# Expert tail of a two-block kernel: last down slabs in column halves, residual kept aside, one input slab loaded later

## The chip, the cores and the metric

The kernel runs on one core of one Trainium2 chip. Its time is the device time of one execution in microseconds (us), and the number compared is the median of several executions. Engines: PE (TensorE), DVE (VectorE), ACT (ScalarE), POOL (GpSimd) and SP (SyncE); the last two issue most of the DMA transfers. Each engine works through its own instructions in the order written.

## The reference, cut to what matters

Two transformer blocks run one after the other on 256 tokens of width 1024, in float32. The first ends in a mixture of 32 experts, top 2 per token:

```python
a = jnp.einsum('nd,edf->nef', t, w_gate)          # 32 experts, 1024 -> 256
b = jnp.einsum('nd,edf->nef', t, w_up)
hid = jax.nn.silu(a) * b * combine[:, :, None]
routed = jnp.einsum('nef,efd->nd', hid, w_down)   # 256 -> 1024
ffn = routed + shared
h = h + rms_norm(ffn, post_ffn_norm)              # end of the first block
...
h = rmsnorm(x, norm_mix_g)                        # start of the second block
proj = h @ w_in                                   # 1024 -> 7168
```

All expert weights (96 slabs of 1 MB: a gate, an up and a down matrix of each expert) are read from memory. Then follow the second block's projections, recurrence, attention, MLP and final norm, none of which the change alters in what they compute.

## The kernel before

**Experts.** They go in eight groups of four (`QUADS`, q = 0 to 7). A group has 12 slabs: four gate, four up, four down. They live in a ring of 12 slots of the big buffer, and slab n may be loaded once the slab 12 before it is used up (`expert_slab_used`). Even slabs are issued on SP's queue, odd ones on POOL's (L442). For each group PE multiplies the gate slabs (L2215, 64 records), the up slabs (L2215), turns the hidden values (L2222), multiplies the down slabs (L2229, 32 records, which write PSUM banks 2 and 3), and adds the result into the sum of the tokens by a matmul with the routing weights (`combine`, L2236, 8 records), after ACT (L935) and DVE (L1563) copied the two banks to `yrow`. `keep_busy` (L2126) are matmuls whose result nobody reads; group 7 has 16 of them between gate and up.

**From the first block to the second.** The token sums lie in PSUM banks 4 to 7, two banks for each half `t` of the tokens. ACT squares them and takes the root (L976, L979); DVE scales by the root and by the norm's weight `gain_ffn` (L1652) and adds the residual, a scaled copy of `h_tok` read with a stride (L1656). That completes `ffn_tmp` and counts up `h_ffn`. ACT squares again (L983), DVE normalizes to `h2n` (L1662), PE transposes it (L2137). ACT and DVE then write the high and low parts of each of eight column chunks (L990 into XH, L1666 into XL), and the second block's first matmuls (L1886 to L1888) start with chunk 0.

**Second block's weights.** They come as 1 MB slabs too, numbered m = 0, 1, ..., in a ring of eight slots, all on SP's queue (L511), where each of the 128 x 8 rows of a slab is one piece of 1 KB. Each slab gives two units. `high2(v)` on ACT (L678) rounds unit v of the weights, `low2(v)` on DVE (L1174) writes what is left. Units 0 and 1 are slab 0, units 2 and 3 are slab 1. ACT rounds unit 2 (`high2(2)`) between the two squares of L983. Slots 0 to 7 of the two rings are the same memory: slot 1 was the last group's second gate slab.

```python
for m in range(RING2):
    sp.wait_ge(ev("expert_slab_used"), RING * (QUADS - 1) + m + ASIDE + 1)
    second_slab(m)
```

Of the kernel before, what the change touches and what calls it, by code (L numbers as in the profile page):

```python
# [17 lines left out]
P = 128  # L18
# [104 lines left out]
def build(nc, A, out):  # L123

    ctx = ExitStack()
    with ctx:
# [7 lines left out]
        def const(name):  # L134
# [5 lines left out]
                    "overflow_known", "lambda_abs", "ple_root"),  # L140
            scalar=("meta_std", "router_high", "mix_std", "group_exp", "pair_exp", "lambda_exp"),
            tensor=("angles", "kpe_swapped", "mix_sums", "routed", "ranks", "expert_totals"))
# [120 lines left out]
        gain_ffn = ar(2048, D)  # L263

# [178 lines left out]

        def expert_slabs(queue, parity):
# [10 lines left out]
            for n in range(RING + ASIDE + parity, QUADS * RING, 2):  # L455
                queue.wait_ge(ev("expert_slab_used"), n - RING + 1)
                expert_slab(queue, n)
# [7 lines left out]
        def _(sp):  # L465
# [33 lines left out]
            expert_slabs(sp, 0)  # L499

# [45 lines left out]
        def _(pool):  # L546
# [70 lines left out]
            pool.dma_start(gain_mix, broadcast(A["post_mix_norm"][0])).then_inc(ev("gain_mix_loaded"), 16)  # L617
# [7 lines left out]
            pool.dma_start(gain_ffn, broadcast(A["post_ffn_norm"][0])).then_inc(ev("gain_ffn_loaded"), 16)  # L625
# [23 lines left out]
            for gain, name in ((gain_mlp, "norm_mlp_g_2"), (gain_ple, "norm_ple_g_2"), (gain_final, "norm_final_g_2")):  # L649
                v = A[name] if name == "norm_final_g_2" else A[name][0]  # L650
                pool.dma_start(gain, broadcast(v)).then_inc(ev("gains_loaded"), 16)
# [5 lines left out]
        def _(act):  # L657
# [203 lines left out]
            junk2 = junk.rearrange("p (b n) -> p b n", b=2)  # L861
# [68 lines left out]
            def rows_of(q):  # L930

                act.wait_ge(ev("expert_slab_used"), (q + 1) * RING)
# [14 lines left out]
            turned_weights(0)  # L947
            for q in range(1, QUADS):
# [11 lines left out]
            act.wait_ge(*mark("overflow_known"))  # L960
            more = act.value_load(overflow[0:1, 0:1], min_val=0, max_val=1)
            with act.If(more > 0):
# [1669 lines left out]
```

## Time and profile before

| | us |
|---|---|
| median of 3 runs | 881.74 (880.6 to 881.96) |
| profiled execution | 879.64 |
| its span | 878.0 |
| PE busy in the span | 797.6 (91%) |
| DVE busy | 482.6 (55%) |
| ACT busy | 383.0 (44%) |
| mean granted TensorE clock | 0.967 of full |

Times of the trace count from the span's start. Busy shares are averages over stages with different limits: the expert stage reads its slabs at the full rate of the DMA queues while PE waits for them, and the second block keeps PE busy nearly throughout. The granted clock is 1.00 at 2.4 GHz and 0.50 at 1.2 GHz. 878.0 is from the first to the last instruction; 1.6 more lie around it.

### The profile page before, as it was taken

The numbers are of one execution on the slowest core, as the hardware profiler recorded it, in microseconds if no ns is written. First come the engines' busy times: TensorE is split into PE (matmuls) and PEld (weight loads), VectorE is DVE, ScalarE is ACT, GpSimd is POOL, SyncE is SP. The second block draws the span as 40 slices with busy tenths as digits, with TensorE's granted clock in tenths as the row PEclk, the third lists the DMA queues.
The fourth block names the chain that finished last, engine by engine and source line by source line (L and its number), as shares of the span: only waits on it lengthen the run. The fifth ranks groups of instructions, "written<-read, shape, count | busy, mean of one in ns | idle before, by whom it ended". The sixth has DMA issues, their size and how long they took to land.

```text
span 878.0 us, 13431 instructions
## 1 busy us (share of the span) xinstructions
PE 797.6 (91%) x5491; PEld 633.9 (72%) x5491; DVE 482.6 (55%) x799; ACT 383.0 (44%) x650; POOL 47.6 (5%) x114
## 2 busy tenths in 40 slices
PE   6997999999568666979999999999999999999995
PEld 5986789675234423459999876678878999999974
DVE  6777658311010030084926787677676666666675
ACT  5574667211000200075457656564344544444454
POOL 5000120011000101000000000000000000000000
PEclk9999999999889888899999999999999999999998
DMA  9960185899999999996428544346555655555101
GB/s 279 375 233 33 50 334 217 330 402 419 421 421 421 420 421 422 402 326 200 140 85 300 192 156 137 103 163 232 172 176 192 191 190 184 181 183 182 43 1 48
DMA packets 77998, 205.81 MB, mean 234 GB/s; under 512 B 5720, under 2 KB 48896, under 8 KB 65648
## 3 DMA queue, kind: packets, MB, share of 16 engines
q1 hardware_dynamic: 69454, 150.44, 48.6%
q0 software_dynamic: 8480, 54.49, 15.3%
q8 instruction: 45, 0.74, 0.3%
q14 instruction: 17, 0.14, 0.0%
q10 hardware_dynamic: 2, 0.00, 0.0%
HBM read 203.87 MB, written 1.05 MB: 233 GB/s over the span
## 4 chain that ended last, share of the span: by engine, by line
PE 69%; DMA 14%; DVE 8%; ACT 6%; issue 3%; SPq 0%; POOL 0%; ACTq 0%; DVEq 0%
DMA big<-in_w_gate 13%; PE ps L2064 11%; PE ps L2065 10%; PE ps L2066 10%; PE ps L1886 8%; PE ps L1888 8%; PE ps L1887 8%; PE ps L2215 6%; PE ps L2191 2%; PE ps L2229 1%; ACT WH L669 1%; DVE WL L1166 1%; PE ps L2434 1%; PE ps L2448 1%; ACT WH L678 1%
## 5 line engine op out<-in xcount | busy, mean ns | idle before, releaser
L1174 DVE TENSOR_TENSOR WL<-big,WH 128x1024 fp32r<-128x1024 f32 x154 | 186.6, 1222 | 95.8 <-ACT WH L678 95.2
L678 ACT ACTIVATE WH<-big 128x1024 fp32r<-128x1024 f32 x154 | 160.4, 1053 | 62.6 <-PE ps L2066 62.1
L1886 PE MATMUL ps<-XH,WH 128*128 128x256 f32 (+1 forms) x640 | 185.1, 289 | 1.0 <-DVE XL L1666 0.5
L1888 PE MATMUL ps<-XH,WL 128*128 128x256 f32 (+1 forms) x640 | 182.7, 285 | 0.0
L1887 PE MATMUL ps<-XL,WH 128*128 128x256 f32 (+1 forms) x640 | 182.6, 285 | 0.0
L1886 PEld LDWEIGHTS ps<-XH,WH 128*128 128x128 f32 x640 | 123.2, 193 | 3.9 <-issue 2.0
L1887 PEld LDWEIGHTS ps<-XL,WH 128*128 128x128 f32 x640 | 123.2, 193 | 0.8
L1888 PEld LDWEIGHTS ps<-XH,WL 128*128 128x128 f32 x640 | 123.1, 192 | 0.0
L2215 PE MATMUL ps<-big 128*32 128x256 f32 x1024 | 75.1, 458 | 38.9 <-DMA big<-in_w_gate 27.4
L2064 PE MATMUL ps<-WH,XH 128*128 128x512 f32 x240 | 99.0, 412 | 1.5 <-ACT big L1001 1.2
L2215 PEld LDWEIGHTS ps<-big 128*32 128x32 f32 x1024 | 41.0, 131 | 73.8 <-issue 61.6
L2065 PE MATMUL ps<-WH,XL 128*128 128x512 f32 x240 | 93.8, 391 | 0.0
L2066 PE MATMUL ps<-WL,XH 128*128 128x512 f32 x240 | 93.7, 390 | 0.0
L1551 DVE TENSOR_TENSOR big<-big,ps 128x256 f32<-128x256 f32 x8 | 3.4, 421 | 120.3 <-ACT big L928 120.2
L2064 PE MATMUL ps<-WH,HH 128*128 128x512 f32 x152 | 59.9, 394 | 0.6 <-DVE HL L1841 0.6
L2065 PE MATMUL ps<-WH,HL 128*128 128x512 f32 x152 | 59.5, 392 | 0.0
L2066 PE MATMUL ps<-WL,HH 128*128 128x512 f32 x152 | 59.3, 390 | 0.0
L2064 PEld LDWEIGHTS ps<-WH,XH 128*128 128x128 f32 x240 | 45.0, 188 | 15.8 <-issue 5.2
L1166 DVE TENSOR_TENSOR WL<-big,WH 128x1024 fp32r<-128x1024 f32 (+1 forms) x39 | 40.5, 1045 | 24.8 <-ACT WH L669 24.6
L2066 PEld LDWEIGHTS ps<-WL,XH 128*128 128x128 f32 x240 | 45.0, 188 | 9.7
L2065 PEld LDWEIGHTS ps<-WH,XL 128*128 128x128 f32 x240 | 45.2, 188 | 7.4
L1116 ACT ACTIVATE HH<-big 128x256 fp32r<-128x256 f32 x32 | 13.4, 417 | 76.1 <-DVE big L1838 76.1
(399 smaller groups left out, 1084.8 us busy)
## 6 DMA issues: line engine op xcount, KB each, us to landing
big<-in_w_in SPq DMA_DIRECT2D x35, 1024.0 KB, 9.5
big<-in_w_gate SPq DMA_DIRECT2D x16, 1024.0 KB, 16.4
big<-in_w_up SPq DMA_DIRECT2D x16, 1024.0 KB, 17.2
big<-in_w_down SPq DMA_DIRECT2D x16, 1024.0 KB, 18.4
big<-in_w_gate POOLq DMA_DIRECT2D x16, 1024.0 KB, 18.4
big<-in_w_up POOLq DMA_DIRECT2D x16, 1024.0 KB, 19.1
big<-in_w_down POOLq DMA_DIRECT2D x16, 1024.0 KB, 19.5
big<-in_w_mlp_up SPq DMA_DIRECT2D x16, 1024.0 KB, 5.5
```

The lines of the kernel that those rows point to most:

```text
L678: s.activation(dst, src, ACT.Copy).then_inc(ev("unit_high"), 1)
L1116: s.activation(HH[:, f % 2, :], zx[:, f % 2, :], ACT.Copy).then_inc(ev("relu_high"), 1)
L1166: v.tensor_tensor(dst, src, h.bitcast(F32), ALU.subtract).then_inc(ev("unit_split"), 1)
L1174: v.tensor_tensor(dst, src, h.bitcast(F32), ALU.subtract).then_inc(ev("unit_split"), 1)
L1886: mm(o, h, rh, start=first, stop=False, skip_group_check=skip)
L1887: mm(o, h, rl, start=False, stop=False, skip_group_check=skip)
L1888: return mm(o, l, rh, start=False, stop=last, skip_group_check=skip)
L2064: mm(o, h, WH[:, b, w], start=first, stop=False, skip_group_check=skip)
L2065: mm(o, l, WH[:, b, w], start=False, stop=False, skip_group_check=skip)
L2066: return mm(o, h, WL[:, b, w], start=False, stop=last, skip_group_check=skip)
L2191: last = mm(o, h_tok[:, t, c * P:(c + 1) * P], sel[:, b, t, first:first + width].bitcast(F32), start=t == 0, stop=t == TT - 1)
L2215: last = mm(ps[j * CAP:(j + 1) * CAP, 1, up * FF:(up + 1) * FF], x(c)[:, j * CAP:(j + 1) * CAP], slabs[j][:, c * FF:(c + 1) * FF], start=c ...
```

## The change

**Last group's down slabs.** Instead of whole slabs, two on each queue, their left column halves (columns 0 to 511) and then their right ones are loaded: slabs 8, 9 and 10 of the group on SP's queue, slab 11 on POOL's. A piece of a half is 2 KB long where a whole slab's is 8 KB. PE multiplies and combines the left half first (`last_down`, `combine(..., (0,))`), then the right half, which goes into banks 3 and 0.

**The norm.** ACT squares the left half of the sums as soon as it is combined; DVE multiplies each half by `gain_ffn` before the root is known; the root's bias is the left half's mean plus EPS. The residual is scaled and reordered by ACT beforehand, in group 7, into slot 1 of the ring (`residual`). The load of the root's function table moves to behind group 7's silu.

**Order.** Because slot 1 holds the residual, slab m = 1 is issued after m = 5 and waits for `h_ffn` to reach 2. `high2(0)` and `high2(1)` move behind the roots, `high2(2)` behind both squares of L983, `low2(0)` and `low2(1)` each behind one half of `h2n`. `keep_busy`: 16 more in group 6 ahead of its down slabs, 6 in place of 16 in group 7, and 16 at once in place of 6 plus 8 at the end. Reading the overflow flag on ACT and DVE moves ahead of group 1; some semaphores are merged.

```diff
+        weighted = lambda t: (ar(3072, D), ar(0, D))[t]
+        residual = lambda t: slot(1)[:, t * D:(t + 1) * D]
...
+        def last_down_halves(queue, slabs):
+            for n in range(2):
+                for k in slabs:
+                    queue.wait_ge(ev("expert_slab_used"), (QUADS - 2) * RING + k + 1)
+                    w = A["w_down"][0][bass.ds((QUADS - 1) * QUAD + k % QUAD, 1)].rearrange("e (p c) n -> p (e c) n", p=P)
+                    cols = slice(n * 512, (n + 1) * 512)
+                    home = expert_home((QUADS - 1) * RING + k).rearrange("p (c n) -> p c n", c=2)
+                    queue.dma_start(home[:, :, cols], w[:, :, cols]).then_inc(last_half(n, k), 16)
...
             expert_slabs(sp, 0)
+            last_down_halves(sp, (8, 9, 10))
...
-            for m in range(RING2):
-                sp.wait_ge(ev("expert_slab_used"), RING * (QUADS - 1) + m + ASIDE + 1)
+            for m in (0, 2, 3, 4, 5, 1, 6, 7):
+                if m == 1:
+                    sp.wait_ge(ev("h_ffn"), TT)
+                else:
+                    sp.wait_ge(ev("expert_slab_used"), RING * (QUADS - 1) + m + ASIDE + 1)
                 second_slab(m)
...
             expert_slabs(pool, 1)
+            last_down_halves(pool, (11,))
...
+                if q == QUADS - 1:
+                    act.wait_ge(ev("expert_slab_used"), q * RING + QUAD)
+                    for t in range(TT):
+                        ins = s.activation(in_order(residual(t)), by_row(h_tok[:, t, :]), ACT.Copy, scale=st(4, t))
+                    ins.then_inc(ev("scalar_mark"), 1)
                 silu_of(q)
+                if q == QUADS - 1:
+                    square_root_ahead(1)
...
-            high2(0)
-            square_root_ahead(1)
+            act.wait_ge(*mark("half_mean"))
             for t in range(TT):
                 act.wait_ge(ev("ffn_summed"), t + 1)
-                s.activation(junk2, ps[:, 4 + 2 * t:6 + 2 * t, :], ACT.Square, accum_out=st(6, t))\
-                    .then_inc(ev("tok_square"), 1)
+                square_part(1, t, st(6, t)).then_inc(ev("tok_square"), 1)
                 act.wait_ge(ev("tok_square"), 2 * TT + t + 1)
-                s.activation(st(7, t), st(6, t), ACT.Sqrt, scale=1.0 / D, bias=EPS).then_inc(ev("tok_std"), 1)
+                s.activation(st(7, t), st(6, t), ACT.Sqrt, scale=1.0 / D, bias=half_mean[:, t:t + 1])\
+                    .then_inc(ev("tok_std"), 1)
+            high2(0)
             high2(1)
...
-                if t == 0:
-                    high2(2)
+            high2(2)
             for c in range(DC):
                 turned(1, c)
...
+            dve.wait_ge(*mark("residual_kept"))
             for t in range(TT):
+                dve.wait_ge(ev("tok_square"), 2 * TT + t + 1)
+                chain(scale_part(1, t))
                 dve.wait_ge(ev("tok_std"), 2 * TT + t + 1)
                 chain(v.reciprocal(st(8, t), st(7, t)))
-                chain(v.scalar_tensor_tensor(out=ffn_tmp[:, t, :].rearrange("p (b n) -> p b n", b=2),
-                                             in0=ps[:, 4 + 2 * t:6 + 2 * t, :], scalar=st(8, t),
-                                             in1=gain_ffn.rearrange("p (b n) -> p b n", b=2),
-                                             op0=ALU.mult, op1=ALU.mult))
-                v.scalar_tensor_tensor(out=in_order(ffn_tmp[:, t, :]), in0=by_row(h_tok[:, t, :]), scalar=st(4, t),
-                                       in1=in_order(ffn_tmp[:, t, :]), op0=ALU.mult, op1=ALU.add)\
-                    .then_inc(ev("h_ffn"), 1)
+                v.scalar_tensor_tensor(out=ffn_tmp[:, t, :], in0=weighted(t), scalar=st(8, t), in1=residual(t),
+                                       op0=ALU.mult, op1=ALU.add).then_inc(ev("h_ffn"), 1)
...
                 if q == QUADS - 1:
                     combine_rows(q - 1)
-                    keep_busy(16, 0)
+                    keep_busy(6, 0)
...
+                if q == QUADS - 2:
+                    keep_busy(16, 0)
...
+            last_down(2, 0, 512).then_inc(ev("tensor_mark"), 1)
             pe.wait_ge(ev("rows_by_scalar"), QUADS)
+            for t in range(TT):
+                last = combine(sel_T[:, 1, 1], t, (0,))
+            last.then_inc(ev("tensor_mark"), 1)
+            pe.wait_ge(ev("last_halves"), 16 * (QUAD - 1))
+            pe.wait_ge(ev("last_half_by_pool"), 16)
+            last_down(3, 512, 768)
+            last_down(0, 768, D).then_inc(ev("expert_slab_used"), QUAD)
...
-            keep_busy(6, 0)
-            pe.wait_ge(ev("h_ffn"), 1)
-            keep_busy(8, 0)
+            keep_busy(16, 0)
             turn_rows(h2n, 1)
```

SP's queue at the end of the experts, before (`in_w_in_2` are the slabs m = 0 to 7 of the second block; a row with x8 is eight transfers one after the other):

```order
L442 DMA big<-in_w_gate 128x2048 [waits expert_slab_used] x2
L442 DMA big<-in_w_up 128x2048 [waits expert_slab_used] x2
L442 DMA big<-in_w_down 128x2048 [waits expert_slab_used] x2
L511 DMA big<-in_w_in_2 128x8x256 [waits expert_slab_used] x8
L506 DMA big<-in_w_rgate_2 128x8x64 [waits unit_split]
```

and in the changed kernel:

```order
L449 DMA big<-in_w_gate 128x2048 [waits expert_slab_used] x2
L449 DMA big<-in_w_up 128x2048 [waits expert_slab_used] x2
L467 DMA big<-in_w_down 128x2x512 [waits expert_slab_used] x6
L537 DMA big<-in_w_in_2 128x8x256 [waits expert_slab_used] x5
L537 DMA big<-in_w_in_2 128x8x256 [waits h_ffn]
L537 DMA big<-in_w_in_2 128x8x256 [waits expert_slab_used] x2
L532 DMA big<-in_w_rgate_2 128x8x64 [waits unit_split]
```

The row that waits for `h_ffn` is slab 1, now the sixth of the eight.

ACT from the first root to the chunks' high parts, before (`slab_in_slot_0` counts the arrival of slab 0, `slab_in_slot_1` of slab 1; XH are the high parts that PE multiplies):

```order
L976 ACTIVATE big,stat<-ps 128x1024 [waits ffn_summed]
L979 ACTIVATE stat<-stat 128x1 [waits tok_square]
L678 ACTIVATE WH<-big 128x1024 [waits slab_in_slot_0,unit_used]
L983 ACTIVATE big,stat<-big 128x1024 [waits h_ffn]
L985 ACTIVATE stat<-stat 128x1 [waits tok_square]
L678 ACTIVATE WH<-big 128x1024 [waits slab_in_slot_1,unit_used]
L983 ACTIVATE big,stat<-big 128x1024 [waits h_ffn]
L985 ACTIVATE stat<-stat 128x1 [waits tok_square]
L990 ACTIVATE XH<-ps,vec 128x256 [waits tok_turned] x4
```

and in the changed kernel:

```order
L1001 ACTIVATE big,stat<-ps 128x512 [waits ffn_summed]
L1028 ACTIVATE stat<-stat,big 128x1 [waits tok_square]
L708 ACTIVATE WH<-big 128x1024 [waits slab_in_slot_0,unit_used] x2
L1034 ACTIVATE big,stat<-big 128x1024 [waits h_ffn]
L1036 ACTIVATE stat<-stat 128x1 [waits tok_square]
L1034 ACTIVATE big,stat<-big 128x1024 [waits h_ffn]
L1036 ACTIVATE stat<-stat 128x1 [waits tok_square]
L708 ACTIVATE WH<-big 128x1024 [waits slab_in_slot_1,unit_used]
L1040 ACTIVATE XH<-ps,vec 128x256 [waits tok_turned] x4
```

The unit of slab 1 still stands ahead of the first XH row, now behind both squares.

## Rows read from the trace of the kernel before

**Rows 1.** The page's 40 slices of the span: PE busy and granted clock.

```profile
PE   6997999999568666979999999999999999999995
PEclk9999999999889888899999999999999999999998
```

**Rows 2.** Chain that ended last, 320 to 400 us: start, length, what.

```profile
327.17 22.98 DMA big<-in_w_gate
350.28 6.34 PE ps L2215 x64
...
360.26 3.65 PE ps L2126 x16
363.91 3.64 PE ps L2215 x64
...
369.55 3.69 PE ps L2229 x32
...
374.26 1.06 ACT WH L678
...
383.08 2.06 DVE big L1656
...
388.67 0.41 DVE XL L1666
389.07 0.14 issue
389.21 0.36 PE ps L1886
```

**Rows 3.** The last four down slabs, 340 to 372 us: issues, and time to landing.

```profile
L442 SPq DMA_DIRECT2D big<-in_w_down x2: 327/380/433, 344.9 to 345.3; - x2
L442 POOL DMA_DIRECT2D big<-in_w_down x2: 527/528/530, 345.1 to 345.7; - x2
DMA to landing us min/median/max: 19.1/21.8/23.8
```

**Rows 4.** DMA totals, 350 to 357 us, expert slabs only.

```profile
DMA packets 397, 2.93 MB, mean 419 GB/s; under 512 B 40, under 2 KB 40, under 8 KB 40
```

**Rows 5.** DMA totals, 374 to 380 us, second-block slabs m only.

```profile
DMA packets 2060, 2.09 MB, mean 349 GB/s; under 512 B 32, under 2 KB 2059, under 8 KB 2059
```

**Rows 6.** DMA rate, 480 to 500 us in 40 slices, slabs in 2 KB pieces.

```profile
GB/s 336 33 0 0 0 0 94 94 262 410 410 406 361 94 0 0 0 29 82 123 369 397 410 406 270 12 0 0 0 82 111 274 389 401 414 365 62 0 0 66
```

**Rows 7.** SP's issues, 377 to 378 us: slab m = 5, the sixth.

```profile
376.97 2.91 SPq L511 DMA_DIRECT2D big<-in_w_in  x1
```

**Rows 8.** DMA issues 377 to 378 us: that slab's time to landing, last column.

```profile
big<-in_w_in SPq DMA_DIRECT2D x1, 1024.0 KB, 12.2
```

**Rows 9.** Stretches: length, then busy PE, PEld, DVE, ACT, POOL; granted clock; DMA.

```profile
344.90:348.90 4.00, 0.00 (x0) 0.00 (x0) 0.68 (x1) 0.58 (x1) 1.57 (x3) 1.00 1.01 420
348.90:350.20 1.30, 0.00 (x0) 0.00 (x0) 0.00 (x0) 0.00 (x0) 0.00 (x0) 0.52 1.06 435
350.20:355.70 5.50, 5.42 (x52) 2.91 (x56) 0.00 (x0) 0.00 (x0) 0.00 (x0) 0.50 1.00 414
400.00:475.00 75.00, 75.00 (x628) 71.83 (x627) 46.13 (x64) 40.08 (x67) 0.00 (x0) 1.00 0.51 175
```

**Rows 10.** Timeline, 362 to 396 us: durations of the steps of the norm.

```profile
373.26 0.60 ACT L935 ACTIVATE big<-ps 128x512 f32<-128x512 f32 x1 [5.31 <-PE ps L2229]
374.10 3.67 PE L2236 MATMUL ps<-big 128*128 128x512 f32 x8 [0.91 <-DVE big L1563]
378.36 1.29 DVE L1652 SCALAR_TENSOR_TENSOR big<-ps,stat,big 128x1024 f32<-128x1024 f32 x1
386.78 0.75 DVE L1662 TENSOR_SCALAR big<-big,stat 128x1024 f32<-128x1024 f32 x1
387.45 1.22 DVE L1174 TENSOR_TENSOR WL<-big,WH 128x1024 fp32r<-128x1024 f32 x1
388.06 3.02 ACT L990 ACTIVATE XH<-ps,vec 128x256 fp32r<-128x256 f32 x8 [1.51 <-PE ps L2137]
```

More of the change, by code:

```diff
@@ L454, in expert_slabs @@
                 expert_slab(queue, n)
-            for n in range(RING + ASIDE + parity, QUADS * RING, 2):
+            for n in range(RING + ASIDE + parity, QUADS * RING - QUAD, 2):
                 queue.wait_ge(ev("expert_slab_used"), n - RING + 1)
@@ L650, in _ @@
                 v = A[name] if name == "norm_final_g_2" else A[name][0]
[L651 removed]
+                pool.dma_start(gain, broadcast(v)).then_inc(ev("rows_loaded"), 16)
         @block.scalar
@@ L947, in _ @@
             turned_weights(0)
+            act.wait_ge(*mark("overflow_known"))
+            more = act.value_load(overflow[0:1, 0:1], min_val=0, max_val=1)
             for q in range(1, QUADS):
@@ L959, in _, with square_part @@
                         .then_inc(ev("scalar_mark"), 1)
-            act.wait_ge(*mark("overflow_known"))
-            more = act.value_load(overflow[0:1, 0:1], min_val=0, max_val=1)
+            def square_part(n, t, into):
+                return s.activation(ar(1024 + 512 * t, 512), ps[:, 4 + 2 * t + n, :], ACT.Square, accum_out=into)
+            act.wait_ge(*mark("half_combined"))
+            square_part(0, 0, half_square[:, 0:1])
+            square_part(0, 1, half_square[:, 1:2]).then_inc(ev("scalar_mark"), 1)
+            act.wait_ge(ev("expert_slab_used"), QUADS * RING)
+            s.activation(yrow[:, 768:D], ps[:, 0, 0:256], ACT.Copy).then_inc(ev("rows_by_scalar"), 1)
             with act.If(more > 0):
@@ L1596, in softplus_of_lambda @@
                 chain(v.tensor_scalar(sc(4), sc(4), -LRU_C, None, ALU.mult))
+            dve.wait_ge(*mark("overflow_known"))
+            more = dve.value_load(overflow[0:1, 0:1], min_val=0, max_val=1)
             for q in range(1, QUADS):
@@ L1615, in _ @@
                     softplus_of_lambda()
-            dve.wait_ge(*mark("overflow_known"))
-            more = dve.value_load(overflow[0:1, 0:1], min_val=0, max_val=1)
+            dve.wait_ge(*loaded("gain_ffn"))
+            for t in range(TT):
+                ins = scale_part(0, t)
+            chain(ins)
             with dve.If(more > 0):
@@ L1662, in _ @@
                 v.tensor_scalar(h2n[:, t, :], ffn_tmp[:, t, :], st(11, t), None, ALU.mult).then_inc(ev("tok_normed"), 1)
-            low2(1)
+                low2(t)
             for c in range(DC):
@@ L2232, in down, with combine @@
                 return last
-            def combine(weights, t):
-                for n in range(2):
+            def combine(weights, t, halves_=(0, 1)):
+                for n in halves_:
                     last = mm(ps[:, 4 + 2 * t + n, :], weights[:, t * P:(t + 1) * P], yrow[:, n * 512:(n + 1) * 512],
@@ L2335, in _, with last_down @@
                     pe.wait_ge(ev("sel_T_ready"), o + 1)
-                wait_slabs(q, 2)
-                down(quad_slabs(q, 2)).then_inc(ev("expert_slab_used"), QUAD)
-            pe.wait_ge(ev("rows_by_scalar"), QUADS)
+                if q == QUADS - 2:
+                    keep_busy(16, 0)
+                if q < QUADS - 1:
+                    wait_slabs(q, 2)
+                    down(quad_slabs(q, 2)).then_inc(ev("expert_slab_used"), QUAD)
+            def last_down(bank, a, b):
+                for f in range(2):
+                    for j in range(QUAD):
+                        last = mm(ps[j * CAP:(j + 1) * CAP, bank, 0:b - a], hidT[:, f, j * CAP:(j + 1) * CAP],
+                                  quad_slabs(QUADS - 1, 2)[j][:, f * D + a:f * D + b],
+                                  start=f == 0, stop=f == 1, skip_group_check=True)
+                return last
+            for k in (8, 10, 11):
+                pe.wait_ge(*slab_e((QUADS - 1) * RING + k))
+            pe.wait_ge(ev("last_slab_1"), 16)
+            last_down(2, 0, 512).then_inc(ev("tensor_mark"), 1)
+            pe.wait_ge(ev("rows_by_scalar"), QUADS)
+            for t in range(TT):
+                last = combine(sel_T[:, 1, 1], t, (0,))
[4 more added lines that the diff above has]
+            last_down(0, 768, D).then_inc(ev("expert_slab_used"), QUAD)
+            pe.wait_ge(ev("rows_by_scalar"), QUADS + 1)
             pe.wait_ge(ev("rows_by_vector"), QUADS)
             for t in range(TT):
-                combine(sel_T[:, 1, 1], t).then_inc(ev("ffn_summed"), 1)
+                combine(sel_T[:, 1, 1], t, (1,)).then_inc(ev("ffn_summed"), 1)
             more = pe.value_load(overflow[0:1, 0:1], min_val=0, max_val=1)
```

60 lines of the change are left out of this document (42 added, 18 removed).

## Prediction

> **What bounds the kernel now.** I read the page's slices first. PE is nearly always busy except in slices 11 to 18, and there the granted clock also falls below full [rows 1]: that is the expert stage. The chain of waits shows why: the last groups hang on the arrival of gate slabs (22.98 us from issue to landing), and PE takes 6.34 us for 64 gate matmuls that it does in 3.64 us for the up slabs a little later [rows 2]. The reader is to see there a stage bound by transfers, in which the queues move 419 GB/s without a break [rows 4].
>
> Next I asked where that bound ends. The last group's down slabs land at latest at 345.7 + 23.8 = 369.5 us [rows 3], and PE begins with them at 369.55 [rows 2]. The transfer was over at the same moment, so all work on PE ahead of 369.5 has no slack to give. From there to 389.21 us, where the second block's first column matmul starts, the chain goes through the two norms [rows 2, 10]. From then on PE is busy without a gap (75.00 of 75 us, clock 1.00) with DVE at 46 and ACT at 40 [rows 9]. So whatever moves the start at 389.21 moves the end by as much, and a slower clock after it is lost for good.
>
> Last I looked at what the transfers do in that stretch, since the change reorders them. The second block's slabs follow on SP's queue without a break, at 349 GB/s: 3.0 us for one of 1.05 MB [rows 5]. The sixth, m = 5, is issued at 376.97 and lands 12.2 us later, at 389.2 [rows 7, 8].
>
> **The change part by part, in the profiled execution (879.64 us, of which 878.0 are the span).**
>
> *Matmuls that nobody reads.* One costs 3.65 / 16 = 0.23 us [rows 2]. 16 more stand ahead of group 6's down slabs: they delay the issue of the last down slabs by 3.65 us from 344.9 [rows 3], when the queues still have the gate and up slabs before them (gate lands at 350.2), so the transfers lose nothing. They shorten PE's idle time before 350.28 to under 2 us, and the gate matmuls may take 3.64 instead of 6.34 us. Ten fewer in group 7 save 2.3 us. Both together would bring PE to its down slabs 5.0 us earlier, at 364.6; the up slabs hold back part of that. None of it counts: what is late next is the down transfer.
>
> *Column halves.* The same 4.2 MB travel, but in pieces of 2 KB. No row has this at the same place. One bound is no cost (8 KB pieces, 419 GB/s, 10.0 us); the other is the price of 1 KB pieces (349 GB/s, 12.0 us), +2.0 us [rows 4, 5]. The nearest row has slabs in 2 KB pieces, whose full slices stand at 390 to 414 GB/s [rows 6]: 10.5 us at 400, so I take +0.5. The 0.5 MB of `gain_ffn` come on POOL's queue after only one slab and so ahead of SP's last halves: +1.2 us for these, nothing for what follows both. The last right half then lands at 369.5 + 0.5 + 1.2 = 371.2, and the left ones some 1.57 MB / 0.41 = 3.8 us before, at 367.4.
>
> *From the halves to the sums.* Left down 1.84 (half of 3.69 [rows 2]) to 369.3, copy 0.60 [rows 10] and its release to 370.0, left combine 1.84 to 371.8, right down to 373.7, the narrower copy some 0.5 to 374.2, and the first half of the right combine 0.92: the first token sum is complete at 375.1, where before it was 374.10 + 1.84 = 375.94 [rows 10]. That is 0.8 earlier.
>
> *The norms.* ACT no longer rounds unit 0 (1.06 [rows 2]) nor loads a function table ahead of the first square. On DVE the pair 1.29 + 2.06 for each half of the tokens [rows 2, 10] becomes a half-width product (about 0.65) and one unstrided add of 1.29. Counting from 375.1: root and reading about 1.0, reciprocal 0.2, add 1.29, with gaps `h_ffn` 1 at 378.1 and `h_ffn` 2 at 380.2. ACT rounds units 0 and 1 in between (2.1) and squares the first half at 379.2 to 380.6. DVE: normalize 0.75 + 0.2 [rows 10] to 381.6, `low2(0)` 1.22 to 382.8, normalize to 383.8, `low2(1)` to 385.0, first XL chunk 0.41, release 0.14: columns could start at 385.6 as far as this path goes. `low2(0)` inside it costs about 0.7, since its old place beside ACT's root is given up. The copies of the residual (two, strided, on ACT, at most 2.06 each if they go like the strided add) lie beside PE's up stage, 8 us long.
>
> *The wait that is added.* Slab 1 is now the sixth on SP's queue and waits for `h_ffn` 2 at about 380.2. SP has issued m = 0, 2, 3, 4, 5 by then, some four of them still to land, so the queue does not run dry and slab 1 lands in the sixth place: 389.2 as m = 5 did before, plus 0.5 for the halves, 389.7. Behind it on ACT stands first the rounding of unit 2, and behind that, in the order in which ACT works, all eight XH chunks, whose transposes are ready by 384.5. PE waits for XH and XL. So: unit 2 rounded 389.75 to 390.8 (1.06), first XH 0.38 (3.02 / 8) to 391.25, first XL 0.41 to 391.7, release 0.14: PE starts at 391.8 in place of 389.21, +2.6 us. In the kernel before the same unit cost nothing, because slab 1 was second in the queue.
>
> The Trainium skill bears on this step (DMA: Bandwidth & Descriptors, "Queues, rings and completion order"): descriptors are consumed in ring order on each DMA engine, yet completion is not in issue order for a queue. Here the slabs are all spread alike and landed 3 us apart in order; by the strict reading slab 1 could overtake only by its last pieces, which changes nothing in the sum.
>
> *The clock.* PE's last work before its wait is the transposes, over by 384.5, since the 16 unread matmuls follow the combine at once and end by 380. That leaves 7.3 us idle. After the 4.0 us without work to 348.9 the granted clock fell from 1.00 to 0.50, and after PE resumed at 350.28 it stayed at 0.50 until 355.7 [rows 9]; the 64 gate matmuls took 2.7 us more than the 64 at full clock [rows 2]. The first columns would run at the 1.2 GHz level likewise. They are paced a little by XL (0.41 a chunk against 0.36 for its three matmuls [rows 2]), which gives back some 0.4; I take +2.1 (ends: 0, and 2.7). Before, this stretch was covered: unread matmuls up to 386.8 and the clock at full when the columns began.
>
> Sum: +2.6 + 2.1 = +4.7 us on the profiled execution, 884.3. The runs shown have a median of 881.74, 2.1 above it; the forecast is given on their scale, 881.74 + 4.7 = 886.4.
>
> Other edits cost nothing: the overflow flag is read while ACT and DVE wait for the experts' transfers, and if that cover were gone it would be two short loads; merged semaphores change no order.
>
> One rule speaks against a term of this sum. DMA: Bandwidth & Descriptors ("Specifications") of the Trainium skill sets the smallest transfer for line rate at 512 B, by which 2 KB pieces cost nothing and the sum would be 0.5 lower, 885.9. The trace does not agree: pieces of 1 KB ran at 349 and those of 8 KB at 419 GB/s [rows 4, 5].
>
> **The rivals.**
>
> *A, the wait is hidden, and the norms' gain shows.* If slab 1 were there before ACT comes to it (by 383), the columns would start at 385.6, 3.6 us earlier: 878.1. This is the faster side. The start follows slab 1's landing by 1.06 + 0.38 + 0.41 and some 0.25 of releases, 2.1 us: a landing before 383.5 hides the wait, one at 387.1 gives the old time, and each later microsecond costs one. For it: the path of the norms is really shorter. Against: five slabs at 3.0 us stand ahead, and the queue was full before and after [rows 4, 5].
>
> *B, the wait holds but the clock does not fall,* or XL's pace covers it: +2.6, 884.3. For it: the clock falls in steps and not always at the same idle time. Against: 4.0 us without work sufficed at 344.9 [rows 9].
>
> *C, 2 KB pieces go as slowly as 1 KB ones,* or two queues of unlike pieces get in each other's way: +2.0 instead of +0.5 on slab 1, 6.2 in all, 887.9. For it: no row has both queues with halves. Against: [rows 6].
>
> **How the numbers follow.** Forecast 0.68, A 0.11, B 0.13, C 0.08. The likeliest gives 886.4; with the clock's term between 1.2 and 2.7 and landing give or take 0.7 its own range is 884.8 to 887.8. To B and C on one scale: 883.4 to 888.2, which leaves out A and some of the tails, under 0.2 together. About 0.2% (1.8 us) is what a measurement of this kernel can tell from no change. Faster by more: A, most of it, 0.10. Within: the rest of A and the lower edge of B (a start at +1.8 or less), 0.09. Slower by more: 0.81.
>
> **What would show it.** In the changed kernel's trace: the last down halves land near 371; the second `h_ffn` comes near 380; ACT's rounding of unit 2 starts only at 389 to 390 with a wait on the transfer of `w_in` of 5 us or so before it, while PE sits idle from 384.5; the first column matmul starts near 391.8 after an XH copy, and the granted clock stands at 0.50 for some 3 to 5 us around it. The column matmuls afterwards are unchanged in number and length. The prediction is wrong if slab 1 lands before 387, if ACT's rounding of unit 2 has no wait, or if PE's columns start before 389.

## The result, and the profile after

| | before | after |
|---|---|---|
| median, same comparison | 880.6 (879.09 to 882.58, 9 runs) | 884.09 (882.14 to 884.78, 9 runs) |
| profiled execution | 879.64 | 884.73 |
| its span | 878.0 | 883.0 |
| mean granted clock | 0.967 | 0.963 |

The ratio (after to before, over all the runs) is 1.0033 with a 95% interval of 1.0021 to 1.0046. The change makes the kernel a third of a per cent slower: 3.5 us in the median, and 5.1 us between the two profiled executions (after's profiled one is near the top of its nine).

The page's slices, to be laid over [rows 1]. The difference that costs time lies in slices 14 to 18 (PE in 14 to 17, the clock in 18). The only other digit that differs is PE's in slice 11, 6 for 5.

```profile
PE   6997999999668759779999999999999999999995
PEclk9999999999889888889999999999999999999998
```

The chain of waits from 341 to 395 us (start, length, what), the counterpart of [rows 2]:

```profile
349.81 16.44 DMA big<-in_w_down
366.25 1.56 issue
367.81 3.67 PE ps L2412 x16
...
372.15 3.78 PE ps L2302 x4
375.93 2.43 PE ps L2412 x32
...
378.96 1.96 PE ps L2302 x4
380.91 5.45 issue
386.37 5.90 PE ps L2192 x16
392.26 1.11 PE ps L2203 x10
393.39 0.48 ACT XH L1040
393.90 0.49 DVE XL L1732
394.39 0.14 issue
394.53 0.35 PE ps L1952
```

L2412 is the down matmul, L2302 the combine, L2192 the unread matmuls, L2203 the transposes, L1952 the second block's first column matmul. It starts at 394.53, where before it started at 389.21: 5.3 us later. The span is 5.0 longer, so all but 0.3 us of that was kept to the end. The reader is to see three things: 16 down matmuls take 3.67 us (L2412) although before 32 took 3.69 [rows 2]; a hole of 5.45 us on PE that ends in no data, only "issue"; and 16 unread matmuls of 5.90 us behind it, on which the transposes wait.

The timeline of the same place (start, length, engine, operation, then in brackets the idle time before it and what ended it) has what the chain leaves out:

```profile
350.28 3.66 PE L2281 MATMUL ps<-big 128*32 128x256 f32 x64 [1.22 <-DMA big<-in_w_gate]
...
359.92 3.66 PE L2281 MATMUL ps<-big 128*32 128x256 f32 x64 [0.96 <-DMA big<-in_w_up]
...
383.98 1.28 DVE L1723 SCALAR_TENSOR_TENSOR big<-big,stat 128x1024 f32<-128x1024 f32 x1
...
390.72 1.06 ACT L708 ACTIVATE WH<-big 128x1024 fp32r<-128x1024 f32 x1 [4.03 <-DMA big<-in_w_in]
...
392.10 1.91 PE L2203 MATMUL ps<-ident,big 128*128 128x128 f32 x16
```

The second `h_ffn` is complete at 383.98 + 1.28 = 385.3. ACT's rounding of unit 2 (L708) waits 4.03 us for slab 1 until 390.7: the wait that the change added is there. But the chain does not run through it, since the transposes begin only at 392.1.

The stretches show the clock (length, then busy PE, PEld, DVE, ACT, POOL; granted clock; DMA), the counterpart of [rows 9]:

```profile
366.90:377.20 10.30, 8.69 (x36) 2.56 (x40) 0.00 (x0) 1.83 (x5) 0.00 (x0) 0.51 1.09 356
384.00:386.40 2.40, 0.03 (x1) 0.03 (x1) 2.36 (x4) 2.31 (x5) 0.00 (x0) 0.50 0.22 72
394.50:400.00 5.50, 5.47 (x44) 5.50 (x45) 5.50 (x10) 4.21 (x9) 0.00 (x0) 1.00 0.78 172
400.00:475.00 75.00, 75.00 (x628) 71.83 (x627) 44.80 (x62) 39.91 (x66) 0.00 (x0) 1.00 0.50 171
```

The clock was at the 1.2 GHz level from 366.9 to 377.2, while PE worked 8.69 of 10.30 us, and again around 385. In the columns it was full, and the stretch from 400 on is as before. The whole loss lies ahead of 394.5.

The transfers. First the issue of slab 1 with its time to landing, the counterpart of [rows 8]:

```profile
big<-in_w_in SPq DMA_DIRECT2D x1, 1024.0 KB, 5.3
```

Then the half slabs (issues, and time to landing), and the totals of 360 to 372 us, the counterparts of [rows 3] and [rows 4, 5]:

```profile
L467 SPq DMA_DIRECT2D big<-in_w_down x6: 540/628/4785, 349.1 to 356.9; - x6
L467 POOL DMA_DIRECT2D big<-in_w_down x2: 731/731/731, 349.4 to 350.1; - x2
...
DMA to landing us min/median/max: 12.3/15.3/16.9
```

```profile
DMA packets 2648, 4.55 MB, mean 379 GB/s; under 512 B 130, under 2 KB 1154, under 8 KB 2647
```

Slab 1 is issued at 385.3, right behind `h_ffn`, and lands 5.3 us later, where m = 5 in a full queue took 12.2 [rows 8]. In the stretch 384 to 386.4 the queues moved 72 GB/s: they had run dry.

### The profile page after: what moved, and what is told of

Read it like the earlier page. It is cut to its first block, busy times and chain, and to the rows that moved or that the text cites. A ratio compares the mean times of both kernels' runs of the same rounds, so it can differ in the third digit from the quotient of the medians.

```text
span 883.0 us, 13497 instructions
## 1 busy us (share of the span) xinstructions
PE 802.4 (91%) x5515; PEld 637.9 (72%) x5515; DVE 481.1 (54%) x802; ACT 388.2 (44%) x657; POOL 48.2 (5%) x114
## 4 chain that ended last, share of the span: by engine, by line
PE 72%; DMA 14%; DVE 6%; ACT 5%; issue 3%; SPq 1%; POOL 0%; ACTq 0%; DVEq 0%
DMA big<-in_w_up 11%; PE ps L2130 11%; PE ps L2131 10%; PE ps L2132 10%; PE ps L1952 8%; PE ps L1953 7%; PE ps L1954 7%; PE ps L2281 5%; PE ps L2257 2%; DMA big<-in_w_down 2%; PE ps L2192 2%; PE ps L2302 1%; PE ps L2295 1%; ACT WH L699 1%; ACT WH L708 1%
## 5 line engine op out<-in xcount | busy, mean ns | idle before, releaser
L708 ACT ACTIVATE WH<-big 128x1024 fp32r<-128x1024 f32 x154 | 160.4, 1053 | 66.0 <-PE ps L2132 61.9
L1952 PE MATMUL ps<-XH,WH 128*128 128x256 f32 (+1 forms) x640 | 185.2, 289 | 1.2 <-DVE XL L1289 0.7
L1952 PEld LDWEIGHTS ps<-XH,WH 128*128 128x128 f32 x640 | 123.3, 193 | 4.0 <-issue 2.9
```

The lines of the kernel that those rows point to most:

```text
L708: s.activation(dst, src, ACT.Copy).then_inc(ev("unit_high"), 1)
L1952: mm(o, h, rh, start=first, stop=False, skip_group_check=skip)
```

## The experiments

The ratio is always to the kernel before on the same chip. Earlier stages shift the expert tail by up to 3.6 us between executions (see "up starts"), so besides the time I compare **D**, the time from the start of the last group's up matmuls to the first column matmul in the profiled execution. After has 394.53 - 359.92 = 34.6. (Before's own up stage waited for PE, so D says nothing there.)

| kernel | ratio, 95% interval | up starts | columns start | D |
|---|---|---|---|---|
| after | 1.0033 [1.0021, 1.0046] | 359.92 | 394.53 | 34.6 |
| e1_slab1_second | 1.0032 [1.0020, 1.0045] | 359.94 | 392.50 | 32.6 |
| e2_few_unread | 1.0042 [1.0027, 1.0056] | 360.25 | 392.99 | 32.7 |
| e3_both | 0.9997 [0.9983, 1.0011] | 357.17 | 387.53 | 30.4 |
| e4_filled_gaps | 1.0029 [1.0019, 1.0040] | 360.27 | 393.25 | 33.0 |
| e5_no_holds | 0.9978 [0.9966, 0.9991] | 359.74 | 386.95 | 27.2 |
| e6_whole_slabs | 1.0052 [1.0035, 1.0070] | 359.75 | 394.19 | 34.4 |
| e8_flag_early | 0.9998 [0.9983, 1.0012] | 360.32 | 390.98 | 30.7 |
| e9_before_unread_moved | 1.0022 [1.0012, 1.0033] | 360.69 | 392.25 | 31.6 |
| e10_unread_ahead_of_flag | 0.9968 [0.9950, 0.9986] | 357.40 | 383.51 | 26.1 |
| e11_slab1_sixth_alone | 1.0031 [1.0018, 1.0044] | 360.74 | 392.73 | 32.0 |
| e12_no_branch_on_pe | 0.9969 [0.9951, 0.9987] | 360.33 | 386.68 | 26.4 |
| e13_whole_slabs_no_holds | 0.9995 [0.9982, 1.0007] | 359.72 | 389.20 | 29.5 |

D comes from one execution of each kernel, so it shows where the time went in that one; what a kernel costs is read from the ratio. A "hold" is from here on a wait that keeps the columns from starting.

My theory from these rows: two holds end at nearly the same time, slab 1 on ACT and the unread matmuls behind PE's hole, and the half clock around the left halves stands ahead of both. In after, ACT is done with slab 1's unit at 391.8, and the first transposes, which had to wait for the unread matmuls, reach it at 393.4. The rival is that one of the two alone costs the time.

**e1: slab 1 second in the queue again.**

```diff
-        residual = lambda t: slot(1)[:, t * D:(t + 1) * D]
...
+        residual = lambda t: ffn_tmp[:, t, :]
...
-            for m in (0, 2, 3, 4, 5, 1, 6, 7):
-                if m == 1:
-                    sp.wait_ge(ev("h_ffn"), TT)
...
+            for m in range(RING2):
```

> Edit on the changed kernel: the residual is kept where the first block's result will stand, so slab 1 is again issued second and waits for nothing; all else as in the changed kernel. Theory T (the columns' start hangs on the last of two things, slab 1 with unit 2, ready for an XH copy at 391.8, and the 16 unread matmuls, which begin only 5.45 us after the last combine at half clock and end at 392.3, so that the transposes come at 392.1): the wait of 4.0 us on ACT goes, the start stays at 394.5, time 884 +- 0.7. Rival R (slab 1's landing alone holds the start, as the prediction had it): start at 390 or before, 4 us faster, 880.

```profile
368.71 3.50 PE L2411 MATMUL ps<-big 128*32 128x512 f32 x16 [3.59 <-issue]
372.93 1.98 PE L2301 MATMUL ps<-big 128*128 128x512 f32 x4 [0.71 <-ACT big L961]
...
383.96 6.27 PE L2191 MATMUL ps<-router 128*128 128x512 f32 x16 [4.59 <-issue]
385.05 1.04 ACT L705 ACTIVATE WH<-big 128x1024 fp32r<-128x1024 f32 x1
390.08 1.91 PE L2202 MATMUL ps<-ident,big 128*128 128x128 f32 x16
```

ACT's wait is gone (no bracket at L705), and the ratio is as after's: taking away the wait alone gives no gain that can be measured. I had expected the columns to start as in after. In this execution D is 2.0 us shorter, mostly for other reasons than the edit: the clock was low for a shorter time (this left combine takes 1.98 us, after's 3.78), which brings the last combine 1.6 us earlier, and the hole is 4.59 us in place of 5.45.

**e2: two unread matmuls at the end in place of 16; e3: both.**

```diff
-            keep_busy(16, 0)
+            keep_busy(2, 0)
```

> Edit on the changed kernel: 2 unread matmuls in place of 16 after the last combine; slab 1 stays sixth. T: transposes come after the second normalize at 388.2, ACT's rounding of unit 2 still ends at 391.8, the columns start at 392.9, 1.6 us earlier, but without the warming matmuls the clock stays at 0.50 for some of the columns and takes 1 to 2.5 us back: 883 to 885. R: the unread matmuls hold nothing, start unchanged, 884 or later by the clock.

> Edit: slab 1 second and 2 unread matmuls. T: both holds are gone, columns start at about 390.0 (second low unit 389.4, XL 0.41), 4.5 us earlier, less 1 to 2.5 us of half clock in the columns: 881 to 882. R: same as the run with slab 1 second, 880.

In e2 the hole is unchanged, the matmuls behind it are over sooner, and the columns wait for slab 1:

```profile
386.74 1.22 PE L2192 MATMUL ps<-router 128*128 128x512 f32 x2 [5.52 <-issue]
...
390.91 1.06 ACT L708 ACTIVATE WH<-big 128x1024 fp32r<-128x1024 f32 x1 [3.92 <-DMA big<-in_w_in]
392.99 0.36 PE L1952 MATMUL ps<-XH,WH 128*128 128x256 f32 x1 [1.81 <-DVE XL L1732]
```

The columns start 1.9 us earlier in D, and the clock then takes it back, as expected: it reads 0.57 to 0.58 between 394 and 398 us, where after's is 1.00.

e1 and e2 each leave the kernel at 1.003 to 1.004. e3, with both edits, is at 0.9997, D shorter by 4.2 us; that is some 2 us better than I had expected. So neither hold carries the loss alone, and the rival falls.

**e4: PE's idle times around the left halves filled** with unread matmuls, the rest as after.

```diff
+            keep_busy(8, 0)
             for k in (8, 10, 11):
                 pe.wait_ge(*slab_e((QUADS - 1) * RING + k))
             pe.wait_ge(ev("last_slab_1"), 16)
             last_down(2, 0, 512).then_inc(ev("tensor_mark"), 1)
+            keep_busy(3, 0)
```

> Edit on the changed kernel: 8 unread matmuls while PE waits for the left halves, 3 more while it waits for the left copy. Theory C (half of the excess lies in the granted clock of 0.50 from 366.9 to 377.2, which makes left down, left combine and right down take 3.64, 3.78 and 2.43 us instead of about 1.8 each): the sums are complete some 4 us earlier, h_ffn 2 at 381 to 382, slab 1 lands at 390 as before since five slabs stand ahead of it, unread matmuls end by 386 at full clock; columns start at 391.8 to 392.2, 2.5 us earlier, 881.5. Rival: the clock falls anyhow, or the idle time and not the clock held this stretch, 884.

```profile
368.18 1.92 PE L2412 MATMUL ps<-big 128*32 128x512 f32 x16
...
370.83 1.96 PE L2302 MATMUL ps<-big 128*128 128x512 f32 x4
...
391.16 1.06 ACT L708 ACTIVATE WH<-big 128x1024 fp32r<-128x1024 f32 x1 [8.13 <-DMA big<-in_w_in]
```

Left down and left combine have their full clock back (1.92 and 1.96 where after has 3.64 and 3.78), the last combine comes 3.7 us earlier, and almost nothing comes of it: ACT's wait grows from 4.03 to 8.13 us, and the ratio, 1.0029, can't be told from after's. I had expected 2.5 us of gain. A gain ahead of a hold turns into waiting.

**e5: e3 and e4 together.**

> Edit on the changed kernel: slab 1 second, 2 unread matmuls at the end, and the two gaps around the left halves filled (8 and 3 unread matmuls). Theory: the sums are complete at 375.3 as in the run with filled gaps, the flag's gap of PE (5.5 us) ends at 382.9, transposes end at about 386 at half clock, columns start at 386.5 to 387.5, two or three us before the kernel before (389.2), less up to 2 us of half clock in the columns: 1 to 2.5 us faster than before, ratio 0.997 to 0.999. Rival: clearing the gaps gives nothing beyond the run with both holds removed, since the flag's gap and the transposes set the start; ratio 1.000.

0.9978: faster than before, as expected. D is 7.4 us below after's. Transposes start at 383.44, columns at 386.95. From e3 to e5 the ratio falls by 0.2% (the two intervals overlap) and D by 3.2 us. Not all of the 3.2 is the clock: left down takes 1.93 in place of 3.64 us, 1.7 less, and its start comes 1.1 us sooner after the up matmuls', because in e3 its transfer was later by that much.

**e6: the last down slabs whole, else as after.** The half-slab loads and their waits are replaced by the old slab loads, and PE waits for all four before the left half.

> Edit on the changed kernel: the last group's down slabs are loaded whole, two on each queue, as in the kernel before; PE's order by left and right half is kept. Theory: the left down begins at 369.5 in place of 367.8 and the clock is at 0.50 for the same matmuls, so the sums come up to 1.7 us later; the right half is there at once, which gives nothing since it was not waited for. Together 0 to 1.7 us slower than the changed kernel, ratio to before 1.004 to 1.006. Rival H (the halves themselves cost, through 2 KB pieces and SP's issues, which took 11 us for six): 1 us or more faster than the changed kernel, ratio 1.003 or less.

Its first down matmul starts at 369.41 (after: 367.81), its columns at 394.19. D is about after's although left down starts later, since the hole was 2.2 us shorter in this execution. 1.0052 against 1.0033, with intervals that overlap. So rival H falls: halves cost nothing here and may gain.

**e9: the kernel before with only its unread matmuls moved** (16 ahead of group 6's down slabs, in group 7 16 down to 6).

```diff
-                    keep_busy(16, 0)
+                    keep_busy(6, 0)
...
+                if q == QUADS - 2:
+                    keep_busy(16, 0)
```

> Edit on the kernel before: only the unread matmuls of groups 6 and 7 as in the changed kernel (16 ahead of group 6's down slabs, 6 for 16 in group 7). Theory: gate matmuls of group 7 take 3.66 in place of 6.34 us, PE comes to its last down slabs earlier and waits for their transfer, which lands as before at 369.5; the longer wait may drop the clock. Ratio 1.000, up to 1.002 with the clock. Rival: the stage hangs on PE after all, 2 us or more faster, ratio 0.998 or less.

```profile
370.93 5.27 PE L2229 MATMUL ps<-big 128*32 128x512 f32 x32 [5.06 <-DMA big<-in_w_down]
```

```profile
367.60:374.40 6.80, 3.47 (x20) 1.01 (x24) 0.00 (x0) 0.00 (x0) 0.00 (x0) 0.51 1.07 359
```

This edit alone costs 0.22%, the upper end of what I had expected. The up matmuls start earlier (360.69, before 363.91), so PE reaches the down slabs early, waits 5.06 us where it had been busy, and the clock is at 0.51 when they come: 5.27 us for what took 3.69 [rows 2]. The columns start 3.0 us later than before, 392.25 against 389.21. The clock makes 1.6 of that. The other 1.4 is the landing of the slabs, after which the down matmuls start at 370.93 and not at 369.55. Whether the edit causes that too is not shown: e6 and e13, which load the same whole slabs behind the same moved matmuls, have 369.41 and 370.90.

**e8: e1 and e4 with PE reading the overflow flag ahead of the groups; e12: the same without flag and branch.** The overflow pass repeats the experts' work for tokens that found no room; with these inputs there are none, the flag is 0 and PE jumps over it. Is the hole on PE the reading of the flag, or this branch?

```diff
+            more = pe.value_load(overflow[0:1, 0:1], min_val=0, max_val=1)
             for q in range(1, QUADS):
...
-            more = pe.value_load(overflow[0:1, 0:1], min_val=0, max_val=1)
             with pe.If(more > 0):
```

> Edit on the changed kernel: slab 1 second, the two gaps filled, the 16 unread matmuls at the end kept, and PE reads the overflow flag ahead of group 1 instead of after the last combine. Theory F (a good part of the 5.5 us between the last combine and the unread matmuls is the read of the flag): the unread matmuls begin 2 to 3 us earlier, near 380, at full clock, end at 384, transposes right behind the second normalize; columns start at 386 at full clock, 3 us before the kernel before: ratio 0.996 to 0.997. Rival G (the gap is the jump over the overflow branch and the fetch of what stands behind it): the gap stays 5 us, the matmuls end at 387 to 388.5, columns start at 390 to 391: ratio 1.001 to 1.002.

> Edit on the changed kernel: slab 1 second, the gaps around the left halves filled, the 16 unread matmuls at the end, and PE without its overflow branch (it leaves out the repeat rounds that a group with more than 32 tokens for one expert would need; these inputs need none). Theory G (the branch and not the flag's read makes the gap): the unread matmuls follow the last combine at once, at full clock, over by 381; transposes follow each normalize at full clock, columns start at 385.6 to 386: 3.5 us before the kernel before, ratio 0.9955 to 0.9965. Rival: some of the gap is left, or the clock falls anyway: ratio 0.998.

e8, then e12:

```profile
375.21 1.96 PE L2301 MATMUL ps<-big 128*128 128x512 f32 x4 [0.64 <-DVE big L1613]
...
381.91 6.80 PE L2191 MATMUL ps<-router 128*128 128x512 f32 x16 [4.75 <-issue]
```

```profile
375.74 1.96 PE L2301 MATMUL ps<-big 128*128 128x512 f32 x4 [0.64 <-DVE big L1613]
377.13 4.25 PE L2191 MATMUL ps<-router 128*128 128x512 f32 x16
...
386.68 0.36 PE L1951 MATMUL ps<-XH,WH 128*128 128x256 f32 x1 [0.53 <-DVE XL L1731]
```

With the early reading a hole of 4.75 us is left, which lies within the 3.27 to 5.93 us of the kernels that read the flag late, so no gain from reading it early is shown. Without the branch no idle time is shown. So what makes the hole is the branch over instructions that are not executed. Both of e8's theories missed in part: its columns start where rival G had them, its ratio lies between the two. With the hole still there, e8's 16 matmuls end late and it is 0.2% behind e5, which has 2. Without the hole they are over at 381.4, before the transposes need PE, and the clock is 1.00 throughout:

```profile
366.00:386.60 20.60, 16.42 (x99) 9.42 (x99) 10.45 (x18) 10.61 (x24) 0.00 (x0) 1.00 1.09 356
```

What goes on in the hole can be seen in the DMA totals, in the queue that brings instructions (packets, MB, share): after, 300 to 400 us, then e12, the same stretch.

```profile
q8 instruction: 7, 0.11, 0.5%
```

```profile
q8 instruction: 5, 0.08, 0.3%
```

The other kernels with the branch have 6 or 7 such packets of 16 KB in this stretch, e12 has 5. In every kernel with the branch one of them begins inside the hole, in narrow windows at 383.8 in after, 383.2 in e6, 380.3 in e3, 379.3 in e8 and 379.0 before; and PE goes on 2.6 to 2.7 us later in all of them. The time from the last combine's end to that packet varies (2.9, 0.7, 3.2, 2.1 and 1.2 us). In e12 none shows between 366 and 390 us. The totals don't say for which engine a packet is; that it comes in PE's hole each time is the evidence. The Trainium skill (Runtime: NRT & Kernel Launch, "Instruction fetch mechanics") says that a taken branch whose target lies outside the pages at hand must fetch the target page before execution goes on. The traces agree, and its price here is 2.6 to 2.7 us; the rest of the hole that sentence does not cover.

**e10: the branch stays, and the unread matmuls stand ahead of the flag's reading** instead of behind the branch; slab 1 second, idle times filled.

```diff
                 combine(sel_T[:, 1, 1], t, (1,)).then_inc(ev("ffn_summed"), 1)
+            keep_busy(8, 0)
             more = pe.value_load(overflow[0:1, 0:1], min_val=0, max_val=1)
...
-            keep_busy(16, 0)
             turn_rows(h2n, 1)
```

> Edit on the run with no holds: in place of 2 unread matmuls behind the overflow branch, 8 ahead of PE's read of the flag, straight after the last combine. Theory (PE's gap of 5.5 us behind the last combine is spent in its sequencer, so matmuls put ahead of it run beside it or push it back by no more than their own 1.9 us): transposes begin between 382.5 and 384.5 at a clock that falls later, columns start at 386 to 387: ratio to before 0.996 to 0.998. Rival: the gap starts only after the last of them, 5.5 us more: transposes at 384.7, columns at 388, ratio 0.999.

```profile
373.72 2.42 PE L2191 MATMUL ps<-router 128*128 128x512 f32 x8
...
379.92 1.25 PE L2202 MATMUL ps<-ident,big 128*128 128x128 f32 x8 [3.77 <-DVE big L1727]
...
383.51 0.55 PE L1951 MATMUL ps<-XH,WH 128*128 128x256 f32 x1
```

```profile
383.50:387.80 4.30, 4.30 (x22) 4.30 (x22) 4.30 (x9) 3.03 (x7) 0.00 (x0) 0.53 1.10 349
```

The 8 matmuls run inside the hole and don't push it back: the instruction packet begins 2.9 to 3.0 us after the last combine, as in e4 and e5, and PE goes on 2.7 us after it, at 379.92. The first half of `h2n` is ready at 379.59, so the hole and the norm now end together; the bracket names the norm, but the hole ends last, by 0.3 us. 0.9968, as fast as e12, which has no branch. This is a complete kernel, and it beats both: 0.3% below before, and by the two ratios 0.65% below after (e10 and after were not run on the same chip). Over e5 (0.9978) its gain is not clear of the intervals. D is 8.5 us below after's. What is left in it is mainly the clock: the first columns run at 0.53.

**e11: e10 with slab 1 sixth and the residual in its slot**, the prediction's mechanism by itself.

> Edit on the run with the unread matmuls ahead of the flag: only slab 1's place goes back to the sixth behind a wait for h_ffn 2, as in the changed kernel, so that its landing is the one hold left. Theory (the prediction's own term): it lands at 390 to 391, five slabs after slab 0, columns start 2.1 us later, near 393, where the other run starts at 386 in the same frame, and the clock falls in PE's wait of 6 us and takes 1 to 2 us from the columns: 6 to 8 us slower than that run, ratio to before 1.003 to 1.005. Rival: the hold gives back most of its time later, ratio 1.001 or less.

```profile
390.64 1.06 ACT L708 ACTIVATE WH<-big 128x1024 fp32r<-128x1024 f32 x1 [5.69 <-DMA big<-in_w_in]
392.73 0.55 PE L1952 MATMUL ps<-XH,WH 128*128 128x256 f32 x1 [4.37 <-DVE XL L1732]
```

```profile
393.00:395.00 2.00, 2.00 (x11) 2.00 (x11) 2.00 (x6) 2.00 (x6) 0.00 (x0) 0.50 1.19 305
```

From 0.9968 to 1.0031, and D from 26.1 to 32.0: with everything else out of the way, this one wait costs 0.6%, some 5.5 us (expected were 6 to 8, and a ratio of 1.003 to 1.005). It is the picture that I had forecast for after: ACT waits 5.69 us, the columns start 2.09 us after slab 1 is there, and they run at 0.50.

**e13: e10 with whole last down slabs**, 15 unread matmuls ahead of them in place of 8.

> Edit on the run with the unread matmuls ahead of the flag: the last down slabs whole, two on each queue, and 15 unread matmuls in place of 8 while PE waits for them; slab 1 second. Theory (halves are worth the 1.3 to 1.7 us by which the left ones land earlier): left down starts at 369.5 in place of 367.8 at full clock, everything behind it 1.3 to 1.7 us later, ratio 0.998 to 0.999. Rival: 2 KB pieces cost what the halves bring, ratio 0.9968 as in that run.

Its first down matmul starts at 370.90 after a wait for the transfer (e10: 365.21, with up matmuls that started 2.3 us earlier), D is 3.4 us longer, and the ratio 0.9995 against 0.9968, the two intervals just overlapping. That is more than I had expected, and some of it is chance: e6, with the same whole slabs, had its first down matmul at 369.41. The halves probably gain, some 2 us by the ratios (e6 to after 0.2%, e13 to e10 0.3%); neither pair is clear of its intervals.

## Why the prediction was right, and where not

**Sign and size.** Forecast +4.7 us to 886.4, range 883.4 to 888.2; measured 884.09, +3.5 in the median, +5.1 between the profiled executions. The start of the columns was the right place to count: +5.3 there, +5.0 in the span. But that the size fits is in good part luck. I had +2.6 in the start, from slab 1 alone, and +2.1 of slow clock behind it; measured were +5.3 in the start, from two holds and a slow stretch ahead of them, and nothing behind it.

**Slab 1.** The step held in its result: landing about 390.6 (forecast 389.7), and ACT waits 4.03 us (5 or so). From landing to the columns I had 2.1 us, which is what e2 and e11 measured; in after it was 3.8, because there the transposes were later still. It was argued through a queue that never runs dry, and that failed: `h_ffn` 2 came at 385.3, not 380.2, the queue was empty, and slab 1 travelled alone in 5.3 us. Two errors, 5.1 us later in the issue and some 4 us shorter on the way, nearly cancelled. With an earlier `h_ffn` the argument is right: in e4 slab 1 was issued at 381.6, took 9.4 us in a full queue and landed no sooner, near 391.1. e11 with e10 shows the wait's price when it stands alone.

**The unread matmuls, "none of it counts".** Wrong. Moving them is 0.22% by itself (e9), and in its trace about half of the delay is the slow clock. I had read only that PE would be early, and not that a PE which is early is idle, and that the clock falls then. Left down, left combine and most of right down ran at half clock: 3.64 + 3.78 + 2.45 = 9.9 us where my steps had 5.5. With the landing 0.4 later that makes the first token sum complete at 379.9 and not at 375.1.

**"The 16 unread matmuls follow the combine at once and end by 380."** Wrong, and the trace of before had it: there too a gap on PE stood between combine and unread matmuls.

```profile
374.10 3.67 PE L2236 MATMUL ps<-big 128*128 128x512 f32 x8 [0.91 <-DVE big L1563]
...
381.69 5.07 PE L2126 MATMUL ps<-router 128*128 128x512 f32 x14 [3.92 <-issue]
```

I had costed instructions by the data that they need, and this gap needs none. In the kernel before it cost next to nothing: the matmuls ended at 386.8 and the second half of `h2n` came at 387.5. In after, matmuls of this kind stand in the way until 392.3, four us later than the second half of `h2n` (388.2), and the clock is at 0.50 for the first four of their 5.9 us. e2 and e3 show this second hold, e12 the cause of the gap in front of it.

**The clock, +2.1.** Not there: the columns ran at 1.00. PE was not idle from 384.5 up to them, as I had it: from 386.4 it worked through the unread matmuls without a gap, and the clock came back to full in their last two us. The low clock lay at 366.9 to 377.2 and from 384 to about 390.4, where I had none, and there it cost more than 2.1: 4.4 us in the first stretch alone (9.9 for 5.5, as above). The forecast place is right for a kernel whose only hold is slab 1 (e11).

**The norm's path.** Right: from the first token sum to `h_ffn` 2 I had 5.1 us, measured 385.3 - 379.9 = 5.4; before it was 383.08 + 2.06 - 375.94 = 9.2 [rows 2, 10]. The gain of 3.8 us is real. Rival A had the columns at 385.6 if nothing held them; e10, moved to after's up start, gives 359.92 + 26.1 = 386.0. A holds its gain only if nothing stands in front of the columns: it fails for this kernel and describes the repaired one.

**Transfers.** The left halves were there by 367.8 (forecast 367.4), the last right half at 371.7 (forecast 371.2). Rival C does not show: 379 GB/s over a stretch in which 1024 of 2648 packets are the second block's 1 KB pieces (1154 under 2 KB, less the 130 under 512 B) lies well above the 349 of these alone [rows 5]. The rate of halves alone no row shows. So the limit of 512 B, which the prediction took from the Trainium skill (DMA: Bandwidth & Descriptors, "Specifications"), and my +0.5 stay undecided between them.

**What stays open.** In after the clock was low for 10 us around the left halves, in e1, with the same matmuls there, for some 3.4. Three of after's nine times lie at 882.1 to 882.5 and the rest at 883.4 to 884.8, which would fit such a difference. That was not shown, since only one execution of a kernel has a trace, and the mean clocks of the nine don't settle it: two of the three short ones are at the top with 0.969 and 0.968, the third is at the bottom with 0.961. It may also be why the profiled execution lost 5.1 us and the median 3.5.

## What to carry to other kernels

Count the holds in front of the point that sets the end, and not only the one that a change adds: where two end within two microseconds, undoing either gave nothing that could be measured (e1 1.0032, e2 1.0042, both 0.9997), and a real gain ahead of them (e4, 3.7 us) turned into waiting. For PE it is not free to come early to a step that waits for a transfer, because it may then do that step at half clock (e9). And look in the trace for idle time that ends in no data: work that is there to fill time belongs ahead of a branch, not behind it (8 matmuls ahead, e10: 0.9968; 16 behind, e8: 0.9998).

## What the runs showed of the hardware

- A jump on PE over a long block that is not executed: a hole of 3.3 to 5.9 us in the kernels that have it (5.45 in after, 3.92 before, 3.27 in e6, 5.93 in e3), none without it (e12). 2.6 to 2.7 us of it follow the start of a 16 KB instruction packet; what decides the 0.7 to 3.2 us before that was not measured. Matmuls put ahead of the branch run inside the hole and don't lengthen it (e10: 5.63 us from the last combine to the transposes).
- A 1 MB slab in 1 KB pieces lands after 12.2 us in a full queue (m = 5, before) and after 5.3 us in an empty one (m = 1, after). Issued at 381.6 (e4), 383.6 (e11) or 385.3 (after), slab 1 landed at 391.1, 390.6 and 390.6: a late issue costs less than its delay.
- The granted clock fell in or just behind gaps of PE of 2.71 (after), 3.77 (e10) and 5.06 us (e9). With 8 and 3 unread matmuls in the gaps (e4) it stood at 1.00, and the down and combine matmuls took 1.92 and 1.96 us against 3.64 and 3.78. These 11 matmuls took 2.12 + 0.96 = 3.1 us of PE's idle time and gave back 3.7. They are no guarantee: in e11, with the same 11, the clock read 0.71 and 0.68 in the stretches 366.4 to 369.2 and 369.2 to 372.0, and left down took 2.76 us.
